# Position rows by product, a 13th weight slot, and the second norm's residual added on TensorE

## The reference

```python
for l in range(DEPTH):                       # DEPTH = 2
    proj = x @ w_in[l]                       # 1024 -> all head groups
    ...                                      # three token mixers: GLA, SSD, RWKV-7
    x = layer_norm(ALPHA * x + heads_out @ w_out[l], ln1_g[l], ln1_b[l])
    ffn = grouped_moe(x, router_w, router_b, w_gate[l], w_up[l], w_down[l])
    x = layer_norm(ALPHA * x + ffn, ln2_g[l], ln2_b[l])

def grouped_moe(...):                        # 16 experts of width 512
    ...                                      # best group of four, top 2 experts in it
    for e in range(16):
        he = silu(h @ w_gate[e]) * (h @ w_up[e])
        out = out + gate[:, e:e+1] * (he @ w_down[e])
```

## Time and profile before

| | us |
|---|---|
| median of 3 runs | 906.67 (904.73 to 909.14) |
| the profiled execution | 906.64 |
| its span in the profile | 904.8 |
| TensorE busy | 820.6 (91%) |
| VectorE busy | 324.4 (36%) |
| ScalarE busy | 180.0 (20%) |
| moved by DMA | 245.83 MB, mean 272 GB/s |

### The profile page before, as it was taken

How to read it: one execution, slowest core, us unless ns; L and a number is a source line. 1 busy time by engine, 2 the same in 40 slices (tenths; PEclk the granted TensorE clock), 3 DMA queues, 4 the chain that set the end, 5 groups by cost and what they waited for, 6 DMA issues and landing times. The chain is left out here.

```text
span 904.8 us, 12776 instructions
## 1 busy us (share of the span) xinstructions
PE 820.6 (91%) x5333; PEld 462.5 (51%) x5333; DVE 324.4 (36%) x675; ACT 180.0 (20%) x374; POOL 25.9 (3%) x102
## 2 busy tenths in 40 slices
PE   5999999977999999988589998999599999999882
PEld 4888566545435443333278876654363354433330
DVE  1186456464211111111333965282822211111015
ACT  0143323322201110000122323241231011100001
POOL 7100000000000000000000000000000000000000
PEclk9999999997999999999879999999799999999996
DMA  9744300259899999999935522020979999999981
GB/s 298 267 172 159 119 20 2 93 227 367 335 392 423 420 392 407 421 420 421 391 95 186 181 99 95 2 95 0 389 290 398 404 421 420 385 422 420 422 347 49
DMA packets 54226, 245.83 MB, mean 272 GB/s; under 512 B 8356, under 2 KB 11280, under 8 KB 29584
## 3 DMA queue, kind: packets, MB, share of 16 engines
q1 hardware_dynamic: 49824, 239.41, 66.7%
q0 software_dynamic: 1344, 4.72, 1.5%
q10 hardware_dynamic: 2992, 0.79, 0.4%
HBM read 243.85 MB, written 1.05 MB: 271 GB/s over the span
## 5 line engine op out<-in xcount | busy, mean ns | idle before, releaser
L524 PE MATMUL bank<-ring,xg 128*64 128x512 f32 x736 | 172.7, 611 | 12.9 <-DMA ring<-in_exp_w_up 12.9
L984 PE MATMUL bank<-x_cm,ring 128*128 128x256 f32 x576 | 129.9, 388 | 5.1 <-DMA ring<-in_w_in 4.2
L984 PEld LDWEIGHTS bank<-x_cm,ring 128*128 128x128 f32 x576 | 111.8, 195 | 22.4 <-issue 5.5
L524 PEld LDWEIGHTS bank<-ring,xg 128*64 128x64 f32 x736 | 55.3, 140 | 110.4 <-issue 107.0
L748 DVE TENSOR_TENSOR y_lo<-bank,y_hi 128x512 fp32r<-128x512 f32 x32 | 22.1, 691 | 207.1 <-ACT y_hi L673 207.1
L524 PE MATMUL bank<-ring_more,xg 128*64 128x512 f32 x256 | 58.4, 597 | 2.0 <-issue 2.0
L733 DVE TENSOR_SCALAR x_cm<-bank,g_col 128x512 f32<-128x512 f32 x32 | 24.0, 751 | 99.4 <-issue 91.9
L554 PE MATMUL bank<-ring,x_cm 128*64 128x512 f32 x256 | 58.1, 593 | 0.0
L991 PE MATMUL bank<-ring,x_cm 128*128 128x512 f32 x128 | 57.7, 599 | 0.0
L673 ACT ACTIVATE y_hi<-bank 128x512 fp32r<-128x512 f32 x32 | 19.1, 597 | 193.6 <-PE bank L554 193.6
L1320 PE MATMUL bank<-ring,x_cm 128*128 128x512 f32 x128 | 55.6, 592 | 0.0
(11 more groups left out here) (366 smaller groups left out, 914.4 us busy)
## 6 DMA issues: line engine op xcount, KB each, us to landing
ring<-in_exp_w_gate SPq DMA_DIRECT2D x48, 1024.0 KB, 11.3
ring<-in_exp_w_up SPq DMA_DIRECT2D x48, 1024.0 KB, 13.4
ring<-in_exp_w_down SPq DMA_DIRECT2D x32, 1024.0 KB, 13.5
ring_more<-in_exp_w_down SPq DMA_DIRECT2D x28, 1024.0 KB, 14.0
ring<-in_w_in SPq DMA_DIRECT2D x24, 1024.0 KB, 9.3
ring_more<-in_exp_w_gate SPq DMA_DIRECT2D x16, 1024.0 KB, 10.5
ring_more<-in_exp_w_up SPq DMA_DIRECT2D x16, 1024.0 KB, 12.6
ring<-in_w_out SPq DMA_DIRECT2D x8, 1024.0 KB, 6.2
```

The source lines that it names most:

```text
L524: m = T.matmul(b[SL * i:SL * i + SL, :], xg[g][:, 4 * h + k, cols], w[:, k, :], start=(h == 0 and k == 0), stop=(h == 1 and k == 3))
L984: m = T.matmul(out_, w[:, k, c:c + n], x_cm[:, k, :], start=(k == 0), stop=(k == KD - 1))
```

## The change

1. **Position rows.** `pos_rows` is gone. In each step TensorE makes the one row that is needed, behind the turn (`position_row`), and VectorE compares it straight from PSUM, now ahead of `product`.
2. **Slots and order.** The freed memory becomes a fifth slot of `ring_more`, and the two that are used once come before `ring_more` in the cycle. `hidden(n+1, 0)` comes before the gathers inside a step; `he` has two buffers. Gate and up of the last expert load before down of the one before it, and TensorE does all of the last expert's hidden products in step 14.
3. **Residual.** In step 14 TensorE adds alpha*x into banks 0 to 3 with four products by `ident_a`, alpha times the identity. The second norm reads its banks in PSUM: VectorE's statistics, in layer 0 ScalarE's standardizing of tile 0 and VectorE's of tile 1, in the last layer VectorE's output passes.
4. **The start.** The 19 small loads move from ScalarE's queue to SP's, behind four weight loads. ScalarE takes half of the first copies to `x_cm`. TensorE multiplies the identity 14 times while it waits for x, and three times more after the turn.
5. **Dummies.** `keep_busy` gives seven products of 128x256 between the router's logits and its selection and three ahead of the first gathers. What they write is not used.

```diff
-    MORE = 4
+    MORE = 5
...
         for e in range(NE):
-            yield from gate_up(e, 1)
             if e + 1 < NE:
+                yield from gate_up(e, 1)
                 yield from gate_up(e + 1, 0)
+            if e + 2 == NE:
+                yield from gate_up(e + 1, 1)
             yield from down(e)
...
-            cycle = [(at + i) % NSLOT for i in range(NSLOT)] + [NSLOT + i for i in range(MORE + ONCE)]
+            cycle = [(at + i) % NSLOT for i in range(NSLOT)] + [NSLOT + MORE + i for i in range(ONCE)]
+            cycle += [NSLOT + i for i in range(MORE)]
...
-        pos_rows = sb("pos_rows", [P, NE, S], mybir.dt.bfloat16)
...
-        he = x_cm[:, 3].rearrange("p (b s) -> p b s", b=FB)
+        he = [x_cm[:, 3 + i].rearrange("p (b s) -> p b s", b=FB) for i in range(2)]
...
+            def position_row(n):
+
+                e = n // rounds
+                mark(T.matmul(b_hid[n % 2][:, 0:S], ident_r[0:NE, e:e + 1].to_broadcast([NE, P]), pos_t[:],
+                              start=True, stop=True), "t_prow")
...
-                hidden(n, 1)
-                if n == 0:
-                    position_rows(0)
-                else:
+                if n < N - 1:
+                    hidden(n, 1)
+                if n:
                     scatter(n - 1)
-                turn(n)
+                if n < N - 1:
+                    turn(n)
+                    position_row(n)
+                turn_of_group = bool(behind) and n % GU == GU - 1
+                if n + 1 < N and not turn_of_group:
+                    hidden(n + 1, 0)
+                if n == N - 2:
+                    hidden(N - 1, 1)
+                    turn(N - 1)
+                    pe.wait_ge(*done("v_x1", l))
+                    for j in range(TT):
+                        for hf in range(2):
+                            T.matmul(bank[2 * j + hf][:], ident_a[:], x_tm[:, j, BCOL * hf:BCOL * hf + BCOL],
+                                     start=False, stop=False)
+                    position_row(N - 1)
...
             def turned_pick(n):
 
                 e, r = divmod(n, rounds)
+                dve.wait_ge(*at("t_prow", n + 1))
                 if n:
                     dve.wait_ge(*at("t_scat", n))
...
-                mark(V.tensor_scalar(pick_t[:], pos_rows[:, e, :], slot_col[:, r:r + 1], None, ALU.is_equal), "v_pick_t")
+                mark(V.tensor_scalar(pick_t[:], b_hid[n % 2][:, 0:S], slot_col[:, r:r + 1], None, ALU.is_equal), "v_pick_t")
...
+                if n == 4:
+                    load_small()
...
+            def keep_busy(b, n):
+
+                for i in range(n):
+                    T.matmul(bank[b][:, 0:S], ident[:], level_mask[:, 0:4], start=True, stop=True)
...
                 if l == 0:
+                    pe.wait_ge(pool_step, 3)
+                    for i in range(14):
+                        T.matmul(bank[0][:, 0:P], ident[:], ident[:], start=True, stop=True)
                     pe.wait_ge(x_loaded, 16 * TT)
-                    pe.wait_ge(pool_step, 3)
                     turn_x(0)
+                    pe.wait_ge(*done("v_x", 0, 1))
+                    for i in range(3):
+                        T.matmul(bank[4][:, 0:S], ident[:], x_tm[:, 0, 0:S], start=True, stop=True)
...
+                keep_busy(1, 7)
                 pe.wait_ge(*done("v_sel", l))
...
+                keep_busy(1, 3)
                 pe.wait_ge(*done("v_first", l))
...
                     else:
                         dve.wait_ge(*done("t_scat", l))
-                    cs = slice(hf * 512, hf * 512 + 512)
-                    do(V.scalar_tensor_tensor(out=x_tm[:, j, cs], in0=x_tm[:, j, cs], scalar=ALPHA,
...
-                    c.add(V.bn_stats(bn6[:, j, hf, :], x_tm[:, j, cs]))
+                        c.add(V.bn_stats(bn6[:, j, hf, :], bank[2 * j + hf][:]))
...
+                            ins = V.tensor_scalar(x_tm[:, j, BCOL * hf:BCOL * hf + BCOL], bank[2 * j + hf][:],
+                                                  bn2[:, j, 0:1], bn2[:, j, 1:2], ALU.subtract, ALU.mult)
...
+                        ln_rstd(1, 0)
+                        act.wait_ge(*done("v_nmean", l))
+                        act.wait_ge(*done("s_rstd", l, 3))
+                        do(A.activation(neg_mean[:, 1:2], neg_mean[:, 0:1], ACT.Copy, scale=bn2[:, 0, 1:2]))
+                        for hf in range(2):
+                            ins = A.activation(x_tm[:, 0, BCOL * hf:BCOL * hf + BCOL], bank[hf][:], ACT.Identity,
+                                               scale=bn2[:, 0, 1:2], bias=neg_mean[:, 1:2])
...
+                        ln_rstd(1, 1)
```

More of the change, by code:

```diff
@@ L624, in experts_t @@
                     slot_gates(g)
-                turn_of_group = bool(behind) and n % GU == GU - 1
-                if n + 1 < N and not turn_of_group:
-                    hidden(n + 1, 0)
-                if n == 0:
-                    position_rows(1)
                 if rounds == 1:
@@ L673, in y_high @@
                 mark(A.activation(y_hi[:], b_y[:], ACT.Copy), "s_yhi")
-            def row_copies(part):
-                act.wait_ge(*done("t_prow", l, part + 1))
-                for i in range(2):
-                    e = NE // 2 * part + 2 * i
-                    ins = A.activation(pos_rows[:, e:e + 2, :].rearrange("p e s -> p (e s)"), bank[i][:], ACT.Copy)
-                inc(ins, "s_prow")
             if rounds == 1:
@@ L1416, in x_entry @@
                     for j in range(TT):
-                        for i in range(4):
+                        for i in (0, 2):
                             dve.wait_ge(*done("t_x", l, 4 * j + i + 1))
```

153 lines of the change are left out of this document (80 added, 73 removed).

## The result

| | median of 6 runs, us | lowest to highest | ratio to before, 95% interval |
|---|---|---|---|
| before | 907.95 | 904.73 to 909.14 | |
| after | 902.25 | 897.64 to 903.42 | 0.9936 (0.9918 to 0.9953) |

The change makes the kernel 0.64% faster: 5.7 us, where 15.5 were forecast. The profiled execution of after took 903.42 us; its span is 901.6, against 904.8 before. So the traces have 3.2 us to account for. From before to after they divide like this: -5.0 up to the first gathers of layer 0, -1.6 and -1.4 in the first gathers of the two layers, +5.5 and +5.7 in the expert stages, -1.5 between the layers, -2.0 in the mixer part of layer 1, and -2.9 behind the last scatter.

The account below looks back on a forecast made before the run. The kernel was taken as a row of stages, each bound by TensorE or the weight stream. Start 5.2, layers 2.6 + 2.6, norms 2.4 + 2.7 make 15.5 us off 906.64: 891.1 us, range 885.5 to 899.0.

Parts of the forecast that it names:

- The start: Up to the first projections: small loads behind weight loads gain 3.0 us, warming TensorE 2.2; 5.2 us in sum.
- The last norm: Last layer's norm: VectorE no longer forms alpha*x + y in four passes, 2.4 us gained.
- rival (d): Norms: bn_stats from PSUM takes 1.4 us instead of 0.69, 2.8 more in each norm, 896.7 us; chance 0.04.
- The norm of layer 0: Between the layers: tiles turned earlier, first projection at 456.2 instead of 458.90, 2.7 us gained.
- The first gathers: Start of each expert stage: dummies keep TensorE's clock up, 1.3 us gained a layer.
- part 2: Expert stage's weight stream: 13th slot and TensorE's changed schedule end the stream 2.9 us earlier a layer.
- Rival (b): Expert stage: the 13th slot brings nothing, new order pinches at load 23; 2.5 us less a layer, 896.1; chance 0.10.
- The end of a layer: Tail of each layer: norm starts 11.5 us after the stream's end, plus 0.7 for waits; 1.6 us lost.
- (c): Clock survives short waits and layer 1 starts at full clock (2.1 us): 4.3 us more gained, 886.8; chance 0.12.
- Case (f): Several shortfalls together, of the weights at the start, the slot and part of the tail: about 902 us; chance 0.06.
- (a): Start: weights land no sooner because their own packets set the pace; 3.0 us less gained, 894.1; chance 0.12.
- (e): Tail of each layer runs at 1.2 GHz, making the kernel slower, up to 924 us; chance 0.04.

Follow-up runs that it names:

- e3: The kernel before with only the new start (small loads on SP, 17 filler products, ScalarE's share of the copies): 900.50 us, ratio 0.9923.
- e4: The kernel before with only the keep_busy filler products added: 905.04 us, ratio 0.9970.
- e10: The kernel before with the new start and the keep_busy filler: 904.83 us.
- e7: The kernel after with the old expert stage (rows in two blocks, 12 slots, old order), residual products ahead of the last hidden product: 894.51 us, ratio 0.9850.
- e13: e6 with 12 slots instead of 13: 905.48 us.
- e2: The kernel after with the 13th slot taken away again (12 slots): 912.05 us, ratio 1.0045 to before.
- e6: The kernel after with the old order of the last two experts and the residual's products ahead of the last hidden product: 897.29 us, ratio 0.9892 to before.
- e16: e7 unchanged, run again: 895.75 us.
- e15: e7 with the first group's slot gates spread over the last three first gathers: 894.40 us, ratio 0.9854 to before.
- e14: e7 without the keep_busy filler: 900.49 us.

## Why the prediction was wrong

- **The start** was right: 5.0 us against 5.2, and e3 keeps them to the end. The first projection starts at 11.2 to 12.0 in all kernels with the new start, and at 14.94 and 14.61 (e4) without it. No run moves the small loads alone, so how much of it is theirs isn't shown.
- **The last norm** was right: 2.9 us against 2.4. bn_stats from PSUM takes 0.65, so rival (d) falls. The Trainium skill (VectorE: DVE Perf Modes, Why PSUM operands drop a tier) holds for the single-source standardizing, 1.53 us for two halves from PSUM against 0.81 from SBUF.
- **The norm of layer 0** gave 1.5 us, not 2.7. The term that failed is the turn of tile 0, forecast 3.9 us behind the norm's start and measured 5.35. The two ScalarE passes took 1.45 us, not 1.2, and ended at 449.85, but the turn starts only at 451.23, 5.4 us behind the scatter as in before (5.5). What TensorE waits for in these 1.4 us isn't in the profile; an instruction transfer ended at 449.77 (see e10). The gain of 1.5 us is tile 1, which is turned right behind tile 0.
- **The first gathers** were right: 4.24 and 4.50 us to the first hidden product instead of 5.87. That a fall of the clock would follow later, behind the slot gates, was in no part of it.
- **The failed step is part 2**, the sentence that TensorE would be "0.95 us earlier at expert 3 and 0.4 at the ninth". By its own 0.14 us a row the ninth would be 0.25. In the trace TensorE starts the first hidden product 5.9 us earlier than before (653.17 against 659.12) and expert 8's first 0.8 us later (779.00 against 778.16): 6.8 us lost in eight steps. Two slow groups are 3.4 of them (5.3 instead of 3.6 us each), the waits for the g-multiply (forecast 0.85), the gate column and pick_t 0.92, 0.33 and 0.64. The position rows took 2.5 us for eight, where the two blocks took 2.23 for sixteen and 1.1 was forecast; the turns, which now stand ahead of a row and no longer ahead of a gather, took 0.7 more, and 0.5 is spread over the rest. The forecast priced a row at 0.14, what one costs in a block; beside other work it is 0.31 to 0.37. For n from 8 on each step is longer by such a row: 12.57 us instead of 12.25. What the new order saves comes later: its waits for weights are 1.1 us instead of 5.6, and the two slow groups behind the longest of these waits in before are gone. So over a whole layer the clock isn't the difference (four falls in after, three in before). e7 against e13 prices rows and order at 3.4 to 5 us a layer.
- **The slot** was sized too small, not too large: 3.3 to 4.9 us a layer (e2, e13), where the forecast had 2.5 at most for the slot itself. Rival (b), the pinch at load 23, is seen in the trace (192 GB/s at 685 to 690) but isn't what decides. Slot and rows came as a pair, as one takes the other's memory, and together they gain nothing: e6 is 1.5 to 2.8 us slower than e16 and e7, of which 1.2 stand between the layers.
- **The end of a layer** was right in its own length: from the last hidden product's start, 868.53, to the norm it took 21.8 us, forecast 21.5 and 0.7 for waits. Wrong was to judge it only against the stream's end. The norm starts 12.5 us behind the last landing, where 12.2 was forecast. The old order with the residual in the gap is 2.3 to 2.5 us a layer better (e6). The slack that the forecast left with the stream was the place for these products.
- **The rivals.** Of (c) the half on layer 1 came true: it starts at full clock in after, and its mixer part is 2.0 us shorter, where (c) had 2.1. It is so in 6 of the 14 traces with the new norm and in none of the 4 with the old one, so it is a chance that came up in the profiled execution, and without it the trace of after would be 1.2 us shorter than that of before, not 3.2. Case (f), about 902, hit the time, but as the sum of shortfalls in (a), (b) and (e), none of which happened, so the hit is luck. (e), a tail at 1.2 GHz, didn't occur: the down products after 1.6 us of waiting kept 3.6 us.

The balance by layer: rows and order +3.4 to +5 (forecast -1, as far as TensorE goes), slot -3.3 to -4.9 (forecast -2 to -2.5), end of the layer +2.4 against the old order with the residual in the gap (forecast +1.6 against before), filler -1.7 and a fall of +1.7 now and then. That is -1 to +4 for the stage with its first gathers, where -2.6 was forecast; the trace of after has +3.8 and +4.3. The split between the clock and the rest is only known within about 2 us, as the falls differ from execution to execution.

e7 and e15 are 1.5% faster than before and 0.9% faster than after: they have all that was right in the forecast, with the expert stage left as it was.

## What to carry to other kernels

A short product costs what it holds up the next one, not what it takes in a row of its like: read the distance between starts at a place where it stands alone. When a step is made longer by little things, count them against the slack of the stage (here 5.6 us of waits for weights) before giving the same stage a gain from the other side. Work that must be added belongs into a wait that the profile shows, here ahead of the product that waits for the last weights; in e6 that product then ran at 3.6 us and not at 5.35.

## What the hardware showed that was not expected

TensorE's granted clock fell to 0.50 while the engine was busy all the time, right behind 32 products of one column (2.03 us); the next 16 full products took 5.3 us instead of 3.6, then the clock was back. It also fell where no slot gates are: in e7 it was 0.56 from 138 to 141, in the mixer part of layer 0, with TensorE busy for 2.94 of 3.00 us. Between executions of one kernel these falls come and go, and the time follows: e7 took 891.15 us at a mean clock of 0.983 and 896.59 at 0.970.

TensorE can stop for 3.5 to 4.3 us in the middle of 16 equal turns, with nothing named that it waits for (e10, e14). In both, a 16 KB instruction transfer ended 1.3 to 1.4 us before it went on. The kernels without the stop that were compared (e3, e16) differ from these two only in the filler, which stands elsewhere. Two parts that each gain (6.9 us and 2.4 us) gave 3.0 us together, and 4.1 of the 6.3 us that are missing are this stop, so a part's worth should be read from its own stretch of the trace beside the total.
